# Spatial mixing of a gated MLP in three passes over high and low parts, with ScalarE, Pool and VectorE making the parts

## What is computed

```python
z = jax.nn.gelu(h @ w_in)                     # (256, 4096)
u, v = jnp.split(z, 2, axis=-1)
v = layernorm(v, ln_g, ln_b)
v = v.reshape(B, S // 128, 128, 8, 256)       # 2 chunks of 128 tokens, 8 groups of 256 columns
sv = jnp.einsum('gts,bcsgd->bctgd', w_s * causal, v) + b_s.T[None, None, :, :, None]
y = u * sv.reshape(B, S, 2048)
return y @ w_out
```

## Time and profile before

| | |
|---|---|
| median of 3 runs | 1204.36 us (1204.18 to 1205.41) |
| the profiled execution's own time | 1205.48 us |
| its span in the profile | 1203.7 us |
| PE, DVE, ACT, POOL busy, share of the span | 74%, 31%, 19%, 2% |
| TensorE's granted clock, mean | 0.863 of full speed |
| moved by DMA | 460.94 MB, mean 383 GB/s |

### The profile page before, as it was taken

How to read it: one execution, slowest core, us unless ns; L and a number is a source line. 1 busy time by engine, 2 the same in 40 slices (tenths; PEclk the granted TensorE clock), 3 DMA queues, 4 the chain that set the end, 5 groups by cost and what they waited for, 6 DMA issues and landing times.

```text
span 1203.7 us, 17617 instructions
## 1 busy us (share of the span) xinstructions
PE 888.8 (74%) x7843; PEld 507.7 (42%) x7843; DVE 376.7 (31%) x484; ACT 228.5 (19%) x389; POOL 21.9 (2%) x65
## 2 busy tenths in 40 slices
PE   9999999999995556565666666666666666666676
PEld 7788888888442222222222222232222222222232
DVE  5554746444242222222222222222222222222234
ACT  6544655434210000000000000000000000000003
POOL 1100000000200000000000000000000000000000
PEclk9999999999997777777787778787878788787889
DMA  8877667856999999999999999999999999999998
GB/s 279 326 260 255 192 219 246 297 191 251 395 424 431 431 432 431 435 430 431 431 432 433 431 430 432 433 430 430 432 432 434 430 431 432 430 434 430 427 426 336
DMA packets 46166, 460.94 MB, mean 383 GB/s; under 512 B 3912, under 2 KB 4528, under 8 KB 30128
## 3 DMA queue, kind: packets, MB, share of 16 engines
q1 hardware_dynamic: 45184, 457.19, 91.8%
q0 software_dynamic: 864, 3.21, 0.8%
q10 hardware_dynamic: 80, 0.02, 0.0%
HBM read 458.05 MB, written 2.36 MB: 382 GB/s over the span
## 4 chain that ended last, share of the span: by engine, by line
DMA 49%; PE 46%; ACT 2%; DVE 2%; SPq 1%; issue 1%; POOLq 0%; POOL 0%; ACTq 0%; DVEq 0%
DMA low_slots<-in_e_w_up 45%; PE scattered_out L1291 20%; PE bank L1487 12%; PE bank L1578 5%; PE pair L1448 3%; DMA high_slots<-in_e_w_up 2%; PE scattered_out L1591 1%; PE pair L1456 1%; DMA out_h<-acc 1%; ACT arena L733 1%; DMA w_raw<-in_a_w_in 1%; DVE w_lo L845 1%; SPq L421 0%; PE scattered_out L1253 0%; PE bank L1392 0%
## 5 line engine op out<-in xcount | busy, mean ns | idle before, releaser
L1095 DVE TENSOR_TENSOR acc<-scattered_out,acc 128x2048 f32<-128x2048 f32 x58 | 132.9, 2291 | 617.7 <-PE scattered_out L1591 617.7
L1487 PE MATMUL bank<-low_slots,arena 128*32 128x256 f32 x2048 | 153.2, 454 | 146.3 <-DMA low_slots<-in_e_w_up 146.0
L1487 PE MATMUL bank<-high_slots,arena 128*32 128x256 f32 x1952 | 144.7, 453 | 139.6 <-DMA high_slots<-in_e_w_up 139.6
L1487 PEld LDWEIGHTS bank<-low_slots,arena 128*32 128x32 f32 x2048 | 83.8, 126 | 218.0 <-issue 187.6
L1487 PEld LDWEIGHTS bank<-high_slots,arena 128*32 128x32 f32 x1952 | 78.8, 126 | 207.6 <-issue 176.6
L845 DVE TENSOR_TENSOR w_lo<-w_raw,w_hi 128x1024 fp32r<-128x1024 f32 x95 | 117.3, 1234 | 121.8 <-ACT w_hi L565 121.3
L565 ACT CAST w_hi<-w_raw 128x1024 fp32r<-128x1024 f32 x95 | 99.9, 1052 | 132.7 <-PE scattered_out L1291 126.5
L1291 PE MATMUL scattered_out<-w_hi,xT_first 128*128 128x512 f32 x376 | 122.1, 396 | 0.9 <-DVE w_lo L845 0.9
L1291 PE MATMUL scattered_out<-w_hi,xT_second 128*128 128x512 f32 x376 | 121.8, 396 | 0.2 <-DVE w_lo L845 0.2
L749 ACT COPY arena<-bank 128x256 f32<-128x256 f32 x32 | 11.9, 373 | 547.7 <-PE bank L1487 547.7
L1578 PE MATMUL bank<-down_slots,arena 128*32 128x512 f32 x944 | 108.0, 596 | 2.1 <-DMA down_slots<-in_e_w_down 1.4
(11 more groups left out here) (254 smaller groups left out, 514.3 us busy)
## 6 DMA issues: line engine op xcount, KB each, us to landing
down_slots<-in_e_w_down SPq DMA_DIRECT2D x26, 4096.0 KB, 21.1
low_slots<-in_e_w_gate SPq DMA_DIRECT2D x13, 4096.0 KB, 30.5
low_slots<-in_e_w_up SPq DMA_DIRECT2D x13, 4096.0 KB, 39.7
high_slots<-in_e_w_gate SPq DMA_DIRECT2D x13, 4096.0 KB, 30.4
high_slots<-in_e_w_up SPq DMA_DIRECT2D x13, 4096.0 KB, 39.6
w_raw<-in_a_w_in SPq DMA_DIRECT2D x64, 512.0 KB, 3.8
w_raw<-in_a_w_out SPq DMA_DIRECT2D x32, 512.0 KB, 4.5
down_slots<-in_e_w_down SPq DMA_DIRECT2D x6, 2048.0 KB, 19.3
```

The source lines that it names most:

```text
L1095: dve.tensor_tensor(acc[:, t, :], OUT[:, :], (acc if e else h)[:, t, :], ALU.add).then_inc(acc_done, 1)
L1487: ins = pe.matmul(GU[c * CAP:(c + 1) * CAP, 0:256], rows_k, gate_columns(rows_of[c // 2][k], c % 2), start=(a == 0 and k == 0), stop=(a == ...
```

## The change

- `v_hi` (v rounded to fp32r) and `v_lo` (the remainder), `ws_hi` and `ws_lo` are made of v and of the transposed matrices. `v_lo` takes the place of v, `ws_hi` that of `ws_raw`, `ws_lo` that of `ws_T`. `v_hi` lies where the weights' slot 2 is.
- `mix_v(g)` handles a group for both token tiles at once: three fp32r matmuls of 512 columns, ws_hi·v_hi, ws_hi·v_lo, ws_lo·v_hi.
- ScalarE: the copy of the transposed matrices moves from block 5 to block 4 and becomes `ws_hi`; eight copies `split_v` (128x512) are new, one a half from half 5 of block 5 to half 4 of block 6; the bias is one instruction of 512 columns a half where it was two of 256.
- VectorE: four `ws_rest` of 128x256, after halves 1 and 2 of block 5.
- Pool: eight subtractions of 128x512, `v_lo = v - v_hi`, each as soon as ScalarE's copy is there.
- SP: chunk 2 moves from the end of block 3 to the end of block 10, behind a wait for the last mixing product.

```diff
+        with ExitStack() as mixer:
+            sb("first_slots", [P, 2 * 4096], F32, mixer)
+            v_hi = sb("v_hi", [P, NT, D], F32R, mixer)
@@ SP
-                if 1 <= n <= 3:
+                if 1 <= n <= 2:
                     load_chunk(n - 1)
...
+                if n == 2:
+                    sp.wait_ge(sv_ps, GRP)
+                    load_chunk(2)
@@ Pool
+            for i in range(NT * NB):
+                cols = slice(i // NT * NBLK, (i // NT + 1) * NBLK)
+                pool.wait_ge(mix_hi, GRP // 2 + i + 1)
+                pool.tensor_tensor(v_lo[:, i % NT, cols], v[:, i % NT, cols], v_hi[:, i % NT, cols].bitcast(F32),
+                                   ALU.subtract).then_inc(mix_lo, 1)
@@ ScalarE
+            def split_v(i):
+                cols = slice(i // NT * NBLK, (i // NT + 1) * NBLK)
+                act.wait_ge(ln_done, i + 1)
+                act.copy(v_hi[:, i % NT, cols], v[:, i % NT, cols]).then_inc(mix_hi, 1)
...
                 if hc == 6:
                     act.activation(unused[:, 0:1], eps_col[:, :], ACT.Gelu_apprx_tanh)
+                if hc >= 5:
+                    split_v(hc - 5)
             n = NB + 2
-            hi_half(n, 0)
-            hi_half(n, 1)
+            for hc in range(2):
+                hi_half(n, hc)
+                split_v(hc + 3)
...
             for hc in range(2, HC):
                 hi_half(n, hc)
+                if hc < 5:
+                    split_v(hc + 3)
                 bias_v(hc - 2)
@@ VectorE
+            def ws_rest(i):
+                dve.wait_ge(mix_hi, i + 1)
+                dve.tensor_tensor(ws_lo[:, 2 * i:2 * i + 2, :], X[i % 4][:, 0:2 * P].rearrange("p (g t) -> p g t", g=2),
+                                  ws_hi[:, 2 * i:2 * i + 2, :].bitcast(F32), ALU.subtract).then_inc(ln_step, 1)
+            for hc in (1, 2):
+                lo_half(n, hc)
+                ws_rest(2 * hc - 2)
+                ws_rest(2 * hc - 1)
@@ TensorE
-            def mix_v(i):
-                g, t = i // NT * 2, i % NT
...
-                pe.wait_ge(ln_done, i + 1)
-                if i >= 4:
-                    pe.wait_ge(sv_done, i - 3)
-                for j in range(2):
-                    ins = pe.matmul(X[i % 4][:, j * GD:(j + 1) * GD], ws_T[:, g + j, :],
-                                    v[:, t, (g + j) * GD:(g + j + 1) * GD], start=True, stop=True)
+            def mix_v(g):
+                pe.wait_ge(mix_lo, g // 2 * NT + NT)
+                if g >= 4:
+                    pe.wait_ge(sv_done, g - 3)
+                cols = slice(g * GD, (g + 1) * GD)
+                for part, (a, b) in enumerate(((ws_hi, v_hi), (ws_hi, v_lo), (ws_lo, v_hi))):
+                    ins = pe.matmul(X[g % 4][:, :].rearrange("p (t n) -> p t n", t=NT), a[:, g, :], b[:, :, cols],
+                                    start=(part == 0), stop=(part == 2))
                 ins.then_inc(sv_ps, 1)
```

More of the change, by code:

```diff
@@ L143, in hybrid_layer @@
         with ExitStack() as mixer:
+            with ExitStack() as parts:
+                v_lo = sb("v_lo", [P, NT, D], F32R, parts)
             v = sb("v", [P, NT, D], F32, mixer)
             u = sb("u", [P, 2, NT, NBLK], F32, mixer)
+            with ExitStack() as parts:
+                ws_hi = sb("ws_hi", [P, GRP, P], F32R, parts)
             ws_raw = sb("ws_raw", [P, GRP, P], F32, mixer)
-            ws_T = sb("ws_T", [P, GRP, P], F32, mixer)
+            ws_lo = sb("ws_lo", [P, GRP, P], F32R, mixer)
             xT_first = sb("xT_first", [P, 2, KD // 2, T], F32R, mixer)
@@ L207, in hybrid_layer @@
         v_ready, u_ready, y_done = sem("v_ready"), sem("u_ready"), sem("y_done")
-        ln_step, ln_done, var_done, std_done = sem("ln_step"), sem("ln_done"), sem("var_done"), sem("std_done")
-        wst_ps, wst_done = sem("wst_ps"), sem("wst_done")
+        ln_step, ln_done, std_done = sem("ln_step"), sem("ln_done"), sem("std_done")
+        wst_ps, mix_hi, mix_lo = sem("wst_ps"), sem("mix_hi"), sem("mix_lo")
         sv_ps, sv_done = sem("sv_ps"), sem("sv_done")
         yt_ps, yt_hi, yt_lo = sem("yt_ps"), sem("yt_hi"), sem("yt_lo")
-        sumsq_x_done, ssq_x_done, rms_x_done, rstd_x_done = (
-            sem("sumsq_x_done"), sem("ssq_x_done"), sem("rms_x_done"), sem("rstd_x_done"))
+        sumsq_x_done, stats_done, rms_x_done, rstd_x_done = (
+            sem("sumsq_x_done"), sem("stats_done"), sem("rms_x_done"), sem("rstd_x_done"))
         h_done, sumsq_h_done = sem("h_done"), sem("sumsq_h_done")
@@ L603, in _ @@
                 if hc == 2:
-                    act.wait_ge(ssq_x_done, 1)
+                    act.wait_ge(stats_done, 1)
                     act.activation(rms_x, ssq_x, ACT.Sqrt, scale=1.0 / D, bias=eps_col[:, :]).then_inc(rms_x_done, 1)
@@ L618, in v_block @@
                     hi_half(n, hc)
+                    for i in (2 * hc - 8, 2 * hc - 7) if n == NB and hc in (4, 5) else ():
+                        act.wait_ge(wst_ps, i + 1)
+                        act.copy(ws_hi[:, 2 * i:2 * i + 2, :], X[i % 4][:, 0:2 * P].rearrange("p (g t) -> p g t", g=2)
+                                 ).then_inc(mix_hi, 1)
             for n in range(2, NB + 1):
                 v_block(n, (n - 1) % 2)
+            def split_v(i):
+                cols = slice(i // NT * NBLK, (i // NT + 1) * NBLK)
+                act.wait_ge(ln_done, i + 1)
+                act.copy(v_hi[:, i % NT, cols], v[:, i % NT, cols]).then_inc(mix_hi, 1)
             n = NB + 1
@@ L628, in _ @@
                 hi_half(n, hc)
-                for i in (2 * hc - 8, 2 * hc - 7) if hc in (4, 5) else ():
-                    act.wait_ge(wst_ps, i + 1)
-                    act.copy(ws_T[:, 2 * i:2 * i + 2, :], X[i % 4][:, 0:2 * P].rearrange("p (g t) -> p g t", g=2)
-                             ).then_inc(wst_done, 1)
                 if hc == 2:
-                    act.wait_ge(var_done, NT)
+                    act.wait_ge(stats_done, 1 + NT)
                     act.activation(std_v, v_mean_var[:, :, 1], ACT.Sqrt, bias=eps_col[:, :]).then_inc(std_done, 1)
@@ L638, in _, with bias_v @@
                     act.activation(unused[:, 0:1], eps_col[:, :], ACT.Gelu_apprx_tanh)
+                if hc >= 5:
+                    split_v(hc - 5)
             n = NB + 2
-            hi_half(n, 0)
-            hi_half(n, 1)
+            for hc in range(2):
+                hi_half(n, hc)
+                split_v(hc + 3)
             gelu_block(n - 1, 1, lambda t: u[:, 1, t, :], u_ready)
-            def bias_v(i):
-                g, t = i // NT * 2, i % NT
-                act.wait_ge(sv_ps, i + 1)
-                for j in range(2):
-                    r = act.activation(v[:, t, (g + j) * GD:(g + j + 1) * GD], X[i % 4][:, j * GD:(j + 1) * GD],
-                                       ACT.Identity, bias=bias_s[:, g + j:g + j + 1])
-                r.then_inc(sv_done, 1)
+            def bias_v(g):
+                act.wait_ge(sv_ps, g + 1)
+                act.activation(v[:, :, g * GD:(g + 1) * GD], X[g % 4][:, :].rearrange("p (t n) -> p t n", t=NT),
+                               ACT.Identity, bias=bias_s[:, g:g + 1]).then_inc(sv_done, 1)
             for hc in range(2, HC):
                 hi_half(n, hc)
+                if hc < 5:
+                    split_v(hc + 3)
                 bias_v(hc - 2)
@@ L893, in _ @@
             dve.reciprocal(rstd_v, std_v).then_inc(ln_step, 1)
-            dve.wait_ge(ln_step, NT * NB + 1)
+            dve.wait_ge(ln_step, NT * NB + GRP // 2 + 1)
             def norm_v(i):
@@ L1336, in _ @@
                     column_block(2 * m + i, i)
-            def mix_v(i):
-                g, t = i // NT * 2, i % NT
-                if i == 0:
-                    pe.wait_ge(wst_done, GRP // 2)
-                pe.wait_ge(ln_done, i + 1)
-                if i >= 4:
-                    pe.wait_ge(sv_done, i - 3)
-                for j in range(2):
-                    ins = pe.matmul(X[i % 4][:, j * GD:(j + 1) * GD], ws_T[:, g + j, :],
-                                    v[:, t, (g + j) * GD:(g + j + 1) * GD], start=True, stop=True)
+            def mix_v(g):
[6 more added lines that the diff above has]
+                                    start=(part == 0), stop=(part == 2))
                 ins.then_inc(sv_ps, 1)
```

8 lines of the change are left out of this document (3 added, 5 removed).

## The result

| | before | changed |
|---|---|---|
| median | 1205.04 us (13 runs, 1204.18 to 1206.48) | 1207.83 us (13 runs, 1207.08 to 1211.02) |
| the profiled execution's own time, span | 1205.48, 1203.7 us | 1207.48, 1205.6 us |

The ratio is 1.0024, with a 95% interval of 1.0016 to 1.0032: the change makes the kernel slower, by 2.8 us. The forecast was +0.9 us and its range ended at 1207.4, so the result lies outside it. 0.7 us of the distance are the base: the median of before was 1204.36 in its first 3 runs and is 1205.04 in 13.

What follows compares the result with a forecast made beforehand. The prediction took TensorE to bound the projection stage and the weight stream the expert stage. Its terms, -1.6 - 0.5 + 3.0, summed to +0.9 us: 1205.2 us on the median of 1204.36, range 1201.8 to 1207.4.

Steps and rivals of the forecast that it cites:

- mixing products: Block 6: three fp32r matmuls make a mixing step 0.686 us instead of 0.885, over 8 halves -1.6 us.
- chunk 2: Moved from the queue of weight halves to the end of block 10, it spares TensorE a wait: -0.5 us.
- meetings of Pool and VectorE: Blocks 5 and 6: each Pool subtraction takes 0.92 us from VectorE, six of eight where VectorE is full: +3.0 us.
- table load: Half 6 of block 5: ScalarE's added copy makes the next rounding late, +0.3 us, or hidden if VectorE is later.
- remainders of the matrices: VectorE's four instructions of 0.42 us behind halves 1 and 2 of block 5 fit and cost nothing.
- from block 8 to the end of block 11: After the mixing, what TensorE gains or loses is carried to the end one for one: 0 added.
- slack: Block 5: the round of the w_hi and w_lo buffers takes 2.57 of 2.745 us, leaving 0.175 us a half.
- VectorE's shorter half: Blocks 5 and 6, where pieces are normalised: VectorE was taken to need about 2.70 of 2.745 us a half.
- the mask: Pool's mask of ws_raw at 35.29 us, the one meeting seen; it gave 0.92 us lost by VectorE per subtraction.
- B: Rival: Pool's subtractions cost nothing and only the table load costs; -1.8 us, 1202.6; chance 0.22.
- C: Rival: VectorE shuts Pool out until it rests, so TensorE waits before the first mixing product; +4.3 us, 1208.7; chance 0.10.
- D: Rival: the products are not cheaper, +2.5 us, 1206.9, or the stage moves for another reason; chance 0.08.

Runs made afterwards that it cites:

- from_fourth_later: The changed kernel with ScalarE's copies of pieces 3 to 7 a half later each; 1207.17 us, 2.16 over the kernel before.
- pool_alone: The kernel before with chunk 2 moved and eight unused Pool subtractions of 128x512, both inputs the same tile; 1207.59 us against 1205.01.
- pool_alone_two: The kernel before with chunk 2 moved and eight unused Pool subtractions whose two inputs are different tiles; 3.26 us over the kernel before.
- pool_writes: The changed kernel with Pool filling v_lo with zeros instead of subtracting; 1203.71 us against 1204.98 for the kernel before.
- dve_shifted: The changed kernel with the subtractions on VectorE, pieces 4 to 7 normalised in block 6 and copies from half 7 on; 1203.82 us against 1205.01 before.
- chunk_only: The kernel before with only chunk 2 moved to the end of block 10; 1205.64 us against 1204.98.
- pool_shifted: The changed kernel with pieces 4 to 7 normalised in block 6 and copies from half 7 on, Pool still subtracting; 1205.13 us against 1205.01 before.

## Why the prediction was wrong

By its own terms, in the trace (start taken off):

| term | forecast | trace of the change |
|---|---|---|
| mixing products | -1.6 | -1.3 |
| chunk 2 | -0.5 | -0.50 |
| meetings of Pool and VectorE | +3.0 | +4.1 |
| table load | hidden | hidden |
| remainders of the matrices | 0 | 0 |
| from block 8 to the end of block 11 | 0 | +0.2 |
| sum | +0.9 | +2.5 |

**The step that failed** is the count in the term on Pool: "Six of the eight fall in halves where VectorE is full (5, 6, 7 of block 5 and 0, 1, 2 of block 6), since each comes 0.1 us after ScalarE's copy", with halves 5, 6 and 7 priced at 0.70, 0.875 and 0.875 and the next three at 0.19. It kept each piece in the half in which the program's order has it. But ScalarE waits only for TensorE and for normalised pieces, not for VectorE's remainders. Once VectorE is late, ScalarE is up to 3.8 us ahead of it, and piece 3 met VectorE before the first remainder of block 6. VectorE lost 1.04 + 0.92 + 1.06 + 0.92 = 3.94 us there. From its remainder of half 5 (at 135.38) to that of block 6's half 0 (147.11) are 11.73 us, so 11.73 - 3.94 = 7.79, 2.60 a half, is its own work when it never waits. TensorE's three halves take 8.24; VectorE comes 3.5 us late. TensorE started block 6 at 148.47 instead of 145.91, with 0.88 us gained before (132.44 to 131.56 at half 4 of block 5): 3.44 us late, so there were 0.07 us of slack left. The forecast had 2.45. Its own rule with a fourth meeting gives 2.45 + 0.875 = 3.33, so the count is 0.9 of the 1.0 that is missing at the start of block 6; the price of a meeting (0.985 on average in these four, not 0.92), the smaller slack (0.07, not 0.175) and VectorE's shorter half (2.60, not 2.70) nearly cancel. from_fourth_later takes the fourth meeting away again and gets back what it cost; pool_alone and pool_alone_two show the price. A delay feeds on itself here: this is what a count per half, made in the undisturbed timeline, can't see.

**Right in place and size:** the meetings in block 6. TensorE's halves 0 to 3 take 163.02 - 148.47 = 14.55 us, where 4 x 3.47 = 13.88 is undisturbed: 0.67, forecast 0.57, and with the 3.44 it makes the +4.1 of the table. (VectorE's remainders 153.37 - 149.69 = 3.68 us apart show it too, 0.21 over 3.47.) Right in kind: that Pool gets in between VectorE's instructions and holds up the next for most of its own length (1.09 of a recorded 1.35 us at 149.57). It did so at all seven pieces behind which a further instruction of VectorE stood; the eighth, at 160.46, met the last one in its stretch, and nothing grew. pool_writes and pool_alone show it as the cause. With the 0.92 us from the mask the estimate was low by a tenth; the letter of the rule in the Trainium skill, page "SBUF — State Buffer", section "Who interferes with whom", taken at 1.07, would have been nearer to the 1.03. That section says "for the whole instruction" only of VectorE's 2-port modes, and of two SBUF inputs that they contend; how long the hold lasts here is what the traces show. The same section says that a Pool instruction that only writes does not contend with such a VectorE instruction; pool_writes agrees (0.75 us kept).

**The products** gain 3.63 - 3.47 = 0.16 us a half instead of 0.20: -1.3, which dve_shifted shows bare (-1.27). The step itself is 0.70 us, 0.01 over the forecast (0.686); the rest is that the 12 projection matmuls beside it take 2.77. Operands in two pieces cost nothing that shows.

**The table load** was put at 0.3 if bare, hidden otherwise. It is hidden in the change, since VectorE is later still, and 0.24 in pool_writes. What was missed is its side effect: the copy of piece 1 slips from behind one rounding to just before the next, so that Pool does pieces 1 and 2 back to back, 3.56 us without a pause beside a full VectorE. No run shows that this costs more than two meetings apart.

**The chunk's move** is right in the trace. In its new place a rounding did wait for its half of w_raw (1.74 us at 269.44), and chunk_only, which loses 0.01 us from block 8 to the end, shows that nothing was passed on. **The matrices' remainders** were free (VectorE still waits 0.83 us for ScalarE in the half behind them).

**The rivals.** B (nothing for Pool) is refuted by seven lengthened instructions. C (Pool shut out until VectorE rests) is refuted by TensorE's waits: no mixing product waits for Pool. D had a part: the products gained a fifth less.

The range failed by 0.4 us. Its upper end was stacked on the first three runs' median, 0.7 under that of 13, and on bounds for the price of a meeting, with none for their number. On the median of 13 it would have ended at 1208.1 and held the result, but by luck: its bound was for a dearer meeting, not for a fourth. Its lower end is 0.15 off its own sum (1204.36 - 1.8 - 0.6 - 0.3 = 1201.65, not 1201.8), which bears on nothing.

## What to carry to other kernels

Price an instruction given to an "idle" Pool by what VectorE beside it loses, if both read SBUF with two inputs: here 1.03 us of VectorE for a subtraction that VectorE itself does in 0.61. Then ask in which stretch VectorE has that much room: in pool_shifted even block 6 was too tight, and only VectorE's own subtraction fitted there (dve_shifted). The copies that release Pool must not run ahead of a late VectorE, or the delay draws further meetings into the full stretch; a wait of the feeding engine for the late one would prevent it, which no run here tried. When a delay is forecast, run the order of the engines again with the delay in it, rather than count by the timeline of before.
